# Conv band matrices built on the chip, channel groups in pairs, and the memory attention of chunk 0 between the groups

## What is computed

```
x  = layer_norm(x)
h  = x @ w_in                                # conv value | conv gate | pool input | queries
a  = silu(layer_norm(conv31(a_val * sigmoid(a_gate))))      # causal depthwise, 384 channels
p  = pool_mixer(p_in)                        # trailing means over 2/4/8/16 frames minus the frame, 384 channels
mo = cross attention of 4 heads into 256 memory tokens (mem @ w_mk, mem @ w_mv), 256 channels
x  = layer_norm(alpha * x + concat(a, p, mo) @ w_out)
x  = layer_norm(alpha * x + ffn(x))          # gated MLP with a causal conv of width 3
```

## Time and profile before

| | us |
|---|---|
| median of three runs | 2109.03 (2105.7 to 2114.14) |
| the profiled execution, its own time | 2111.38 |
| its span, first to last instruction | 2109.4 |
| PE busy | 1909.0 (90%) |
| DVE busy | 1477.5 (70%) |
| ACT busy | 962.9 (46%) |
| POOL busy | 225.8 (11%) |
| mean granted TensorE clock | 0.955 of full speed |

### The profile page before, as it was taken

One profiled execution on the slowest core, in us unless ns is written; L12 is line 12 of the kernel. 1 busy time (PEld: TensorE's weight loads), 2 busy tenths in 40 slices (PEclk: granted clock), 3 DMA queues, 4 the chain that ended last, 5 costly groups with the idle time before them and its releaser, 6 DMA issues.

```text
span 2109.4 us, 26448 instructions
## 1 busy us (share of the span) xinstructions
PE 1909.0 (90%) x8680; PEld 1583.9 (75%) x8680; DVE 1477.5 (70%) x1978; ACT 962.9 (46%) x1657; POOL 225.8 (11%) x299
## 2 busy tenths in 40 slices
PE   4899987668999939999999989999999798999997
PEld 3688867556878827888888868888888686887786
DVE  6444015547889737888888888877777866666999
ACT  3111115445556425655565665565556434334321
POOL 1111011000212210222222002000000000000111
PEclk9899998778999969999999999999999999999999
DMA  5322128542343363434333534221223557557443
GB/s 209 135 92 93 46 73 257 157 151 80 127 168 142 110 220 123 141 128 149 139 139 121 188 120 145 109 86 70 89 89 127 174 202 279 180 179 259 170 168 121
DMA packets 171053, 303.53 MB, mean 144 GB/s; under 512 B 13280, under 2 KB 101472, under 8 KB 170976
## 3 DMA queue, kind: packets, MB, share of 16 engines
q1 hardware_dynamic: 170976, 302.56, 41.2%
HBM read 196.60 MB, written 105.91 MB: 143 GB/s over the span
## 4 chain that ended last, share of the span: by engine, by line
PE 54%; DMA 4%; DVE 3%; issue 1%; ACT 1%; SPq 0%; DVEq 0%; ACTq 0%
PE prod_ps L1754 54%; DMA y_scratch<-up_and_out 2%; DVE mov_lo L1936 1%; DMA mov_raw<-wdown_sums_scratch 1%; DMA mov_raw<-x_operands 1%; ACT mov_hi L1801 1%; DVE up_and_out L1970 0%; DVE up_and_out L1967 0%; DMA mov_raw<-in_w_down 0%; DMA mov_raw<-in_ln_b 0%; DMA up_and_out<-x_scratch 0%; DVE sta_lo L1932 0%; ACT sta_hi L1794 0%; ACT prod_ps L1808 0%; DVE up_and_out L1987 0%
## 5 line engine op out<-in xcount | busy, mean ns | idle before, releaser
L1754 PE MATMUL prod_ps<-mov_hi,sta_hi 128*128 128x512 f32 x1848 | 727.4, 394 | 41.1 <-ACT prod_ps L1808 25.5
L1754 PE MATMUL prod_ps<-mov_lo,sta_hi 128*128 128x512 f32 x1848 | 725.0, 392 | 0.0
L1754 PE MATMUL prod_ps<-mov_hi,sta_lo 128*128 128x512 f32 x1848 | 724.5, 392 | 0.0
L1754 PEld LDWEIGHTS prod_ps<-mov_hi,sta_hi 128*128 128x128 f32 x1848 | 350.9, 190 | 120.4 <-ACT prod_ps L1808 27.6
L1754 PEld LDWEIGHTS prod_ps<-mov_lo,sta_hi 128*128 128x128 f32 x1848 | 351.0, 190 | 73.2
L1754 PEld LDWEIGHTS prod_ps<-mov_hi,sta_lo 128*128 128x128 f32 x1848 | 350.5, 190 | 73.2
L1932 DVE TENSOR_TENSOR sta_lo<-sta_raw,sta_hi 128x512 fp32r<-128x512 f32 (+1 forms) x340 | 222.5, 670 | 64.3 <-ACT sta_hi L1794 62.4
L1794 ACT ACTIVATE sta_hi<-sta_raw 128x512 fp32r<-128x512 f32 (+1 forms) x340 | 198.3, 611 | 145.1 <-PE prod_ps L1754 102.3
L250 PE MATMUL wb<-x0t_hi,win_hi 128*128 128x512 f32 x352 | 141.6, 402 | 1.4 <-DVE x0t_lo L340 1.4
L250 PE MATMUL wb<-x0t_hi,win_lo 128*128 128x512 f32 x352 | 139.0, 395 | 0.0
L250 PE MATMUL wb<-x0t_lo,win_hi 128*128 128x512 f32 x352 | 138.8, 394 | 0.0
(11 more groups left out here) (267 smaller groups left out, 2751.3 us busy)
## 6 DMA issues: line engine op xcount, KB each, us to landing
sta_raw<-in_w_up SPq DMA_DIRECT2D x88, 512.0 KB, 4.1
hidden_scratch<-up_and_out SPq DMA_DIRECT2D x44, 512.0 KB, 2.6
y_scratch<-up_and_out SPq DMA_DIRECT2D x16, 1024.0 KB, 7.3
sta_raw<-hidden_scratch SPq DMA_DIRECT2D x32, 512.0 KB, 4.5
up_and_out<-y_scratch SPq DMA_DIRECT2D x16, 1024.0 KB, 4.9
x_operands<-x_operands_out SPq DMA_DIRECT2D x56, 256.0 KB, 4.2
mov_raw<-x_operands SPq DMA_DIRECT2D x14, 1024.0 KB, 6.8
mov_raw<-in_w_down SPq DMA_DIRECT2D x44, 256.0 KB, 4.6
```

The lines of the kernel that those rows point to most:

```text
L1754: last = pe.matmul(psum, w, x, start=(start and k == 0 and i == 0), stop=(stop and k == m - 1 and i == 2), skip_group_check=True)
```

## The change

- The host passes 40 taps for each partition and group (`conv_taps`, 128x960 in one DMA) in place of the ready bands. ACT and DVE split them once into hi and lo. DVE then makes the ten 128x128 blocks (hi and lo, five lags) of a group's bands in one instruction: taps broadcast over channels, times a mask (`same`) that is one on the blocks of the same channel. It has three buffers, and band n waits for the product of group n-3.
- Groups are loaded, split, evacuated and stored in pairs of 16 channels: one DMA load and one store for a pair, `mix_d` now laid out as (1024, 2048), hi and lo of 512 columns, and pool products of 512 columns. Raw tiles and results have four buffers, hi and lo three, and PSUM three banks.
- The mending of the first pool columns moves from DVE to POOL, once for a pair.
- Keys are computed behind pair 4, values behind pair 7 (with w_mv loaded into another buffer), and the attention of chunk 0 is spread over pairs 12 to 21: scores behind 12 and 14, transposes behind 16 and 18, attend behind 20, with their ACT and DVE pieces at pairs 11 to 21.
- After the fold only the conv norm and pool part of chunk 0 remain, with w_out rows 4 to 7 between their steps. Chunk 0's queries are loaded alone at pair 8.
- Queries are stored, and chunks loaded, in phase order: two DMAs instead of one for each, with runs of 128 elements.

```diff
-    dst = mix_d[row:row + D_MEM, (c % 2) * CH:(c % 2 + 1) * CH].rearrange("(t p) s -> p t s", p=P)
-    sp.dma_start(dst, qb[:, :, :]).then_inc(q_stored, 16)
+    for t in range(QT):
+        row = D_CONV + D_POOL + t * P
+        dst = mix_d[row:row + P, :].rearrange("p (r h q) -> p r h q", r=PHASES, h=2)[:, 4 * (c % 2):4 * (c % 2) + 4, c // 2, :]
+        sp.dma_start(dst, qb[:, t, :].rearrange("p (u q) -> p u q", u=TT)).then_inc(q_stored, 16)
...
+        def load_chunk(sp, c, s, k0, k1, landed):
+            for u in range(TT):
+                src = mix_d[k0 * P:k1 * P, :].rearrange("(k p) (r h q) -> p k r h q", p=P, r=PHASES, h=2)[:, :, TT * (c % 4) + u, c // 4, :]
+                sp.dma_start(mc[:, s, k0:k1, u * P:(u + 1) * P], src).then_inc(landed, 16)
...
+            def load_pair(m):
+                if m >= 4:
+                    sp.wait_ge(gx_lo, m - 3)
+                if m >= 4 + CONV_PAIRS:
+                    sp.wait_ge(g_fix, m - 3 - CONV_PAIRS)
+                src = cp_d[m * 2 * GROUP:(m + 1) * 2 * GROUP, :].rearrange("(g c) (r q) -> (c r) g q", g=2, r=PHASES)
+                sp.dma_start(gx_raw[:, m % 4, :, :], src).then_inc(gx_in[m % 4], 16)
...
+            for m in range(CONV_PAIRS, NP):      # on POOL
+                pool.wait_ge(g_out, 2 * m + 2)
+                if m > CONV_PAIRS:
+                    pool.wait_ge(g_fix, m - CONV_PAIRS)
+                edge_link(pool.tensor_tensor(edge[:, :, :], y, x, ALU.add))
+                edge_link(pool.tensor_tensor(edge[:, :, :], edge[:, :, :], factor, ALU.mult))
+                pool.tensor_tensor(y, edge[:, :, :], x, ALU.subtract).then_inc(g_fix, 1)
...
+            for m in range(NP):                  # on PE
+                pair(m)
+                if m == 4:
+                    keys()
+                if m == 7:
+                    values()
+                if m == 12:
+                    pe.wait_ge(kv_lo, 2 * QT)
+                    pe.wait_ge(ident_ok, 3)
+                    scores(0, 0)
+                if m == 14:
+                    scores(0, 1)
+                if m == 16:
+                    turn(0, 0)
+                if m == 18:
+                    turn(0, 1)
+                if m == 20:
+                    attend(0)
...
+            def conv_band(n):                    # on DVE
+                if n >= 3:
+                    dve.wait_ge(g_mm, n - 2)
+                out = gt[n % 3].rearrange("p (e c r) -> p e c r", c=GROUP, r=PHASES)
+                tap = tap_parts[:, n, :, :].rearrange("p e (s o r) -> p (e s) o r", o=1, r=PHASES).to_broadcast((P, 2 * LAGS, GROUP, PHASES))
+                mask = same.rearrange("p (o c r) -> p o c r", o=1, r=PHASES).to_broadcast((P, 2 * LAGS, GROUP, PHASES))
+                dve.tensor_tensor(out, tap, mask, ALU.mult).then_inc(gt_ok, 1)
...
+            for m in range(NP):                  # on DVE
+                conv_band(2 * m + 3)
+                conv_band(2 * m + 4)
+                if m + 3 < NP:
+                    pair_lo(m + 3)
+                if m == 0:
+                    for x in (kt_hi, kt_lo, v_hi, v_lo):
+                        dve.memset(x[:, :, :, :].bitcast(mybir.dt.uint32), 0).then_inc(prep_zero, 1)
+                if m == 1:
+                    prep_low(memT_lo, r_memT, memT_hi, 1)
+                if m == 2:
+                    prep_low(wk_lo, r_wk, wk_hi, 2)
...
+            for m in range(NP):                  # on ACT
+                pair_out(m)
+                if m + 3 < NP:
+                    pair_hi(m + 3)
...
+                if m == 13:
+                    exps(0, 0)
+                if m == 15:
+                    exps(0, 1)
+                if m == 16:
+                    wout_hi(2)
+                if m == 17:
+                    turned_hi(0, 0)
+                if m == 19:
+                    turned_hi(0, 1)
+                if m == 21:
+                    attn_hi(0, 0)
...
-            chunk(0, 0, None)                    # on PE, behind the fold
+            mean(0)
+            variance(0)
...
+            conv_total(0, 0)                     # on DVE, behind the fold
+            deviations(0, 0)
+            wout_lo(4)
+            query_lo(1, 1)
+            square_sum(0)
+            wout_lo(5)
+            scale_conv(0, 0)
+            wout_lo(6)
+            conv_lo(0, 0)
+            pooled_lo(0, 0)
+            wout_lo(7)
```

More of the change, by code:

```diff
@@ L455, in mixing_phase @@
         gx_in = [sem(f"group_in{i}") for i in range(4)]
-        gt_in = [sem(f"taps_in{i}") for i in range(3)]
+        gt_in = sem("taps_in")
         gx_hi = sem("group_hi_done")
@@ L883, in group @@
                         cols = slice(LEAD - s, LEAD - s + QS)
-                        for i, x in enumerate((gx_h, gx_l)):
-                            last = pe.matmul(bank, band_h[:, first + s, :], x[:, slot, cols], start=(s == 0 and i == 0), stop=(s == lags - 1 and i == 1))
-                last.then_inc(g_mm, 1)
+                        for i, x in enumerate((h, l)):
+                            last = pe.matmul(bank, band_h[:, first + s, :], x[:, :, cols], start=(s == 0 and i == 0), stop=(s == lags - 1 and i == 1))
+                    last.then_inc(g_mm, 2)
             def keys():
@@ L920, in _ @@
                     last.then_inc(fold_mm, 1)
-            pe.wait_ge(prep_lo, 4)
-            for t in range(MT):
-                for k in range(KT):
-                    cols = slice(t * P, (t + 1) * P)
-                    for i, (w, x) in enumerate(exact_parts(memT_hi[:, k, cols], memT_lo[:, k, cols], wv_hi[:, k, :], wv_lo[:, k, :])):
-                        last = pe.matmul(ps_t[:, t, 0:D_MEM], w, x, start=(k == 0 and i == 0), stop=(k == KT - 1 and i == 2))
-                last.then_inc(prep_mm, 1)
             pe.wait_ge(fold_lo, 2 * CT)
@@ L1138, in chunk @@
                     turned_x1(before, 0)
-            for t in range(MT):
-                act.wait_ge(prep_mm, QT + t + 1)
-                for h in range(HEADS):
-                    o = (h % 2) * HEAD_DIM
-                    last = act.activation(v_hi[:, t, h, o:o + HEAD_DIM], ps_t[:, t, h * HEAD_DIM:(h + 1) * HEAD_DIM], ACT.Copy)
-                last.then_inc(prep_ev, 1)
-            query_hi(0, 0)
-            chunk(0, 0, None, None)
-            for n in range(CT, KT):
-                wout_hi(n)
+            wout_hi(4)
+            squares(0, 0)
+            query_hi(1, 1)
+            wout_hi(5)
+            deviation(0)
+            wout_hi(6)
+            act.wait_ge(cln_in, 32)
+            swish(0, 0)
+            pooled_hi(0, 0)
+            wout_hi(7)
             chunk(1, 1, 0, None)
@@ L2153, in by_partition, with lag_taps @@
         return np.ascontiguousarray(np.moveaxis(v.reshape(tiles, P, *v.shape[1:]), 0, 1))
-    def lag_bands(w):
-        bands = np.zeros((CONV_GROUPS, GROUP, PHASES, LAGS, GROUP, PHASES), w.dtype)
-        for s in range(LAGS):
-            for r_in in range(PHASES):
+    def lag_taps(w):
+        taps = np.zeros((GROUP, PHASES, CONV_GROUPS, LAGS, PHASES), w.dtype)
+        for r_in in range(PHASES):
+            for s in range(LAGS):
                 for r in range(PHASES):
```

412 lines of the change are left out of this document (222 added, 190 removed).

## The result

The changed kernel took 2089.02 us (median of 4 runs, 2085.44 to 2091.08), the kernel before on the same chip 2109.47 (4 runs, 2105.7 to 2114.14). The ratio is 0.9899, 95% interval 0.9878 to 0.992: 20.4 us faster. The profiled execution took 2091.08 us with a span of 2089.4; its projection ended at 302.9, 1.0 us earlier than before.

A forecast was written before the change was run, and what follows sets the result against it. Before the change it saw conv groups near DMA-bound (share 0.86), pool groups latency-paced and chunk 0 a chain of single instructions. Terms summed to 159.6 us against 185.4, 25.8 less: 2111.4 became 2086, range 2071 to 2104.

The forecast's parts named there:

- conv groups with keys and values: Stage after start-up: PE floor, clock loss and about 13 us of PE stalls behind DVE, together 70 us.
- pool groups with attention: Pool stage: four turns (mending, load, hi, out) of 5.2 us, plus attention pieces and a tail, 44.4 us.
- after the fold: From fold end to scores of chunk 1: a chain of copies, norm steps and low parts, 21.3 us, replacing 43.5.
- The stretch: Last projection matmul to first scores of chunk 1: 159.6 us against 185.4, so 25.8 us less.
- the walk: Band-by-band estimate of conv-stage PE stalls: about 13 us; each microsecond more on a band costs about 17.
- Rivals 3 and 4: Conv bands slow on DVE: 2126 us, chance 0.05; or moderately slow (2.2 to 2.8 us): 2099 to 2109, chance 0.07.
- Rival 2: DVE keeps up better: conv stalls of 13 us shrink to 4, turns stay at 4.5; 2074 us, chance 0.14.
- the floor of 56.7: Least PE time in us for conv groups, keys and values, including 2.4 for half clock at the start.
- Rival 1: Attention doesn't hide in the pool stage and the POOL fix costs 2.5 us: 13 us more, 2099, chance 0.16.
- What is gained is that the values are inside: Conv stage: removed band loads (7.5 MB) buy no shorter stage; the gain is that values run within it.
- what was on the path there and is hidden now: Behind the fold: values 5.9 us, chunk 0's scores, softmax, turns and attend, and most w_out parts leave the path.
- Later chunks: Loads of 1 MB in two DMAs with 512 B runs, covered by chunks of over 30 us: costed at nothing.

The follow-up runs named there:

- e3: Changed kernel with every conv band written twice by DVE, the same product again: 2117.39 us (one run).
- e6: Changed kernel with the four memsets of the key and value tiles made by POOL instead of DVE: 2086.35 us, ratio 0.9881.
- e5: Changed kernel with conv bands ready from the host again, split by ACT and DVE, pairs kept: 2087.69 us, ratio 0.989.
- e7: Changed kernel with POOL copying each raw pool tile's edge columns aside, so loads wait for no mending: 2086.61 us, ratio 0.988.
- e4: Changed kernel with the attention of chunk 0 moved back behind the fold: 2092.64 us, ratio 0.9909.
- e10: e8 plus POOL keeping the edge columns aside, so loads wait for no mending: 2079.33 us, ratio 0.9843.
- e11: e9 plus POOL keeping the edge columns aside, so loads wait for no mending: 2076.92 us, ratio 0.9841.
- e12: Kernel before, with only POOL keeping edge columns aside so loads wait for no mending; mending stays on DVE: 2097.39 us, ratio 0.9942.
- e8: Changed kernel with both the attention of chunk 0 and the values moved behind the fold: 2087.84 us (one run).
- e9: Changed kernel with bands from the host, and values and attention of chunk 0 behind the fold: 2085.5 us, ratio 0.9876.
- e2: The changed kernel run again without an edit: 2087.98 us (one run).
- e1: The kernel before run again without an edit: 2106.26 us (one run).

## Why the prediction was right, and where its reasons were not

**The number.** Terms predicted and measured: start-up 12.9 and 12.3 (from 302.9), conv groups with keys and values 70 and 71.1, pool groups with attention 44.4 and 45.6, fold 11 and 9.9, after the fold 21.3 and 22.6. The sum of 159.6 stands against 161.5. The stretch shrank by 23.9 us, 25.8 were forecast; the time fell by 20.4.

**The band.** 1.49 us, as the line through the three subtractions of the earlier trace rows gave. Its price per microsecond came out at 16.6 (e3; 18.7 against the other profile) where the walk said 17. The Trainium skill's rule that runs of two or more adjacent words keep a port's full rate (Vector Engine (DVE) Microarchitecture Reference, measured stream behaviour) agrees: with runs of 8 words 1280 columns took 1.49 us. Rivals 3 and 4 fall with that.

**DVE in the conv groups.** The stalls are where the walk put them, behind bands and not behind DMAs: 2.65, 1.78 and 1.76 us at 329.6, 335.2 and 340.8, where it had 2.4, 2.1 and 2.1 in pairs 2 to 4, then 3.26 at 362.3 for the 3.5 of pair 7, and only 0.5 later; 9.9 in all against 13. Rival 2, stalls of 4 us, falls with that. PE was busy for the other 61.2 us, 4.5 more than the floor of 56.7, at a mean clock of 0.91: two errors of opposite sign that nearly cancel. That each extra instruction on DVE "comes through" is too simple: adding 1.49 us to each of 24 bands did (e3), taking four memsets out of one place brought nothing clear (e6). Bands from the host empty DVE and give the same length (e5), with stalls of PE in much the same places, so the mask product is not what the stage hangs on at about 70 us. The prediction's sentence that the removed band loads buy no shorter stage is confirmed.

**Pool groups with attention, the step that failed.** I built the 44.4 us as four turns of 5.2 that set the stage, with the attention's pieces added to two of them. The sum was right to 1.2 us and the mechanism wrong. If turns and attention added up, cutting the turns would have shortened the stage. With the turn cut it keeps 45.0 us (e7); with the attention out it has 32.2 (e4). So it is the attention's own chain, passed through queues in which pairs and w_out parts stand between its links, that sets the stage. The turn is the bound only where the attention is not there (e10, e11, e12). The turn's own size was right (5.1 us, e8). But without the attention's pieces, about 15.6, the terms give 28.8 us where e4 had 32.2, and the pieces cost 13.4: two errors of opposite sign, so that the sum came within 1.2 us is luck. Rival 1 came closest in its mechanism, though not in its time of 2099: the attention doesn't hide in the pool stage, while the cost of the fix on POOL was small.

**"What is gained is that the values are inside"; "what was on the path there and is hidden now".** This is the reason that the runs refute. The values cost 4 to 6 us in the conv stage (e8 against e4, e9 against e5) and under 1 behind the fold, where they fill PE while it waits for low parts. The attention pays 13.4 us in the pool stage for 18.4 saved behind the fold. With neither placed between the pairs the stretch is 161.8 us (e8), with host bands as well 160.9 (e9), against 161.5. My sum compared the new layout with the old stage lengths and so booked the pairs' gain to the placements. How the pairs gain is argued from the turn, and fits its measured size. One turn now serves two pairs, which are four of the old groups, where it served two of them, and half as many loads, evacuations and waits go through SP and ACT. Of the 24.5 us by which e9's stretch is shorter, 15.7 lie in the pool stage and 6.6 in conv groups and keys.

**Later chunks.** A chunk is now two loads of 512 KB. Each of them landed in the kernel after as follows (500 to 700 us), against 5.3 us for 1 MB in the earlier trace rows:

```profile
mix_in<-mix_scratch SPq DMA_DIRECT2D x8, 512.0 KB, 4.8
```

None of the larger waits behind them names them, as costed.

**From the stretch to the whole.** The stretch gave 23.9 us and the time 20.4. From the scores of chunk 1 to the end the code is the same, and it took 1620.1 and 1619.6 us in the two profiles before, 1625.0 and 1623.2 in the two after, and 1618.9 to 1624.7 in the others. In the first two profiles the extra us arise in the last phase and the passage to it, not in the chunks; in e2 1.2 us of them lie in the chunks. Neither theory of e1 and e2 fits: this part repeated within 0.5 us in the kernel before and moved by 1.8 in the kernel after. Part of this is scatter between executions, since e11 has 1618.9. Whether some 2 us belong to the change stays open.

**Chances.** Faster by over 0.5% had 0.80 and came. The range held the time.

## What to carry to other kernels

Look in a latency-bound stage for a buffer whose release hangs on a small late step, and copy what that step needs: in the kernel before this alone gave 12.8 us, and no engine's busy time pointed to it. A chain of dependent steps that is placed "between" the items of a pipeline pays at each link for all that stands ahead of it in the in-order queues; here it was not hidden, and only the stage with and without it showed that (45.6 and 32.2 us). When a change has several parts, a sum that comes out right doesn't say which part earned it: only undoing the parts singly and together showed that two of three brought nothing that shows, and that one of these, the placing, was a loss once the turn was cut.

## What was not expected of the hardware

The small POOL instructions have a long upper tail: 128x4 took 0.20 us at the median, but 0.76, 1.32 and 0.67 at most in the kernel after (rows L806 to L808 above), and 1.92 once in e7, where it ran beside two DVE subtractions (413.06 and 414.20 in the fence above). A line of DVE and one of POOL in the kernel after, then that of e7:

```profile
411.61 1.22 DVE L1340 TENSOR_TENSOR wout_lo<-x_out,wout_hi 128x1024 fp32r<-128x1024 f32 x1
```

```profile
411.57 1.32 POOL L807 TENSOR_TENSOR pool_edge<-pool_edge,pool_edge_ratio 128x4 f32<-128x4 f32 x1
```

```profile
413.02 1.92 POOL L818 TENSOR_TENSOR pool_edge<-pool_edge,pool_edge_ratio 128x4 f32<-128x4 f32 x1
```

The long ones end with DVE: 411.57 + 1.32 = 412.89 against 411.61 + 1.22 = 412.83, and 414.94 against 414.89 in e7. In the pool stage of the kernel after, 7 of the 36 instructions of the fix took over 0.4 us, and in e4, e7, e8, e10 and e11 38 of 180. Each of these 45 overlapped a DVE subtraction with both inputs in SBUF and ended 0.04 to 0.07 us after it. None that ran alone or only beside a DVE instruction with an input in PSUM was long; some 20 short ones met such a subtraction only near its start or its end. No run took the DVE instructions away, so this rests on the traces alone, and spans on POOL are rough in a profile.

The shorter PE's pauses for the loads became, the higher was the mean granted clock of the pool stage: 0.55 before, 0.68 with pairs (e9), 0.93 with pairs and kept columns (e11). The same 55 matmuls kept PE busy for 21.1 us in e9 and 16.3 in e11. So the cut pauses also gave back 4.8 us of busy time through the clock.
